# First half of the first weight unit as plain f32 products, and a new order of the first transfers

## The reference, cut to what matters

```python
def _rms_f32(xf, g):
    return xf * lax.rsqrt(jnp.mean(xf * xf, axis=-1, keepdims=True) + EPS) * g.astype(jnp.float32)

def hybrid_mixer(h, w_in, w_gate2, b_gate, g_gla, g_q, g_k, w_out):
    proj = h @ w_in
    cuts = np.cumsum([GLA_DK, GLA_DK, GLA_DV, GLA_DV, GLA_GATE_RANK, SB_D, SB_D])
    gq, gk, gv, gr, glr, sq, sk, sv = jnp.split(proj, cuts, axis=-1)
    ...
# in the first block, layer 0
hn = rms_norm(h, mix_norm[layer])
mix = hybrid_mixer(hn, hy_w_in[i], ...)
```

## Time and profile before

| | |
|---|---|
| median of 3 runs | 1041.45 us (1041.06 to 1042.47) |
| the profiled execution | 1040.92 us |
| its span, from first to last instruction | 1039.1 us |
| PE busy | 98% of the span |
| VectorE, ScalarE, GpSimd busy | 64%, 49%, 7% |
| mean granted clock of TensorE | 0.997 |
| first product of unit 0 | at 10.51 us |

### The profile page before, as it was taken

One profiled execution on the slowest core, in us unless ns is written; L12 is line 12 of the kernel. 1 busy time (PEld: TensorE's weight loads), 2 busy tenths in 40 slices (PEclk: granted clock), 3 DMA queues, 4 the chain that ended last, 5 costly groups with the idle time before them and its releaser, 6 DMA issues.

```text
span 1039.1 us, 15941 instructions
## 1 busy us (share of the span) xinstructions
PE 1013.4 (98%) x6789; PEld 869.5 (84%) x6796; DVE 668.1 (64%) x758; ACT 513.6 (49%) x598; POOL 72.1 (7%) x88
## 2 busy tenths in 40 slices
PE   9999999999999999999999999999999999999996
PEld 6996888888888986988989888899658888888885
DVE  6565578676768776768876666254589765455444
ACT  5567564344446325653544345454467464434434
POOL 0000100000000000001111000000148000000002
PEclk9999999999999999999999999999999999999998
DMA  7642457667664752458788775323000445545551
GB/s 266 214 163 81 153 194 276 230 227 246 211 242 164 230 171 83 163 186 304 284 299 277 269 270 208 122 81 122 1 1 2 151 155 202 191 174 201 176 189 41
DMA packets 33756, 187.60 MB, mean 181 GB/s; under 512 B 3744, under 2 KB 7584, under 8 KB 15136
## 3 DMA queue, kind: packets, MB, share of 16 engines
q1 hardware_dynamic: 25488, 155.08, 43.0%
q0 software_dynamic: 7344, 27.79, 7.5%
q10 hardware_dynamic: 864, 3.87, 1.0%
HBM read 181.61 MB, written 1.05 MB: 176 GB/s over the span
## 4 chain that ended last, share of the span: by engine, by line
PE 87%; DVE 7%; ACT 3%; DMA 2%; issue 1%; SPq 0%; DVEq 0%; ACTq 0%
PE PS L603 11%; PE PS L605 11%; PE PS L604 11%; PE PS L285 10%; PE PS L287 10%; PE PS L286 10%; PE PS L1175 2%; DMA raw<-wstream 2%; PE PS L670 2%; PE PS L668 2%; PE PS L669 2%; PE PS L636 1%; ACT w_hi L268 1%; DVE w_lo L272 1%; PE PS L1409 1%
## 5 line engine op out<-in xcount | busy, mean ns | idle before, releaser
L272 DVE TENSOR_TENSOR w_lo<-raw,w_hi 128x2048 fp32r<-128x2048 f32 x138 | 316.2, 2292 | 191.1 <-ACT w_hi L268 191.0
L268 ACT ACTIVATE w_hi<-raw 128x2048 fp32r<-128x2048 f32 x140 | 267.5, 1912 | 157.9 <-DMA raw<-wstream 68.1
L603 PE MATMUL PS<-w_hi,a_hi 128*128 128x512 f32 x512 | 203.1, 397 | 0.0
L605 PE MATMUL PS<-w_hi,a_lo 128*128 128x512 f32 x512 | 199.8, 390 | 0.0
L604 PE MATMUL PS<-w_lo,a_hi 128*128 128x512 f32 x512 | 199.7, 390 | 0.0
L285 PE MATMUL PS<-a_hi,w_hi 128*128 128x256 f32 (+1 forms) x512 | 154.8, 302 | 0.4 <-DVE a_lo L471 0.4
L286 PE MATMUL PS<-a_lo,w_hi 128*128 128x256 f32 (+1 forms) x512 | 151.6, 296 | 0.0
L287 PE MATMUL PS<-a_hi,w_lo 128*128 128x256 f32 (+1 forms) x512 | 151.6, 296 | 0.0
L605 PEld LDWEIGHTS PS<-w_hi,a_lo 128*128 128x128 f32 x512 | 96.1, 188 | 20.6
L603 PEld LDWEIGHTS PS<-w_hi,a_hi 128*128 128x128 f32 x512 | 96.3, 188 | 19.0 <-DVE w_lo L272 0.3
L604 PEld LDWEIGHTS PS<-w_lo,a_hi 128*128 128x128 f32 x512 | 96.4, 188 | 18.3
(11 more groups left out here) (375 smaller groups left out, 1401.8 us busy)
## 6 DMA issues: line engine op xcount, KB each, us to landing
raw<-wstream SPq DMA_DIRECT2D x141, 1024.0 KB, 4.8
modraw<-wmod POOLq DMA_DIRECT2D x48, 512.0 KB, 4.9
U<-CU SPq DMA_DIRECT2D x28, 142.0 KB, 2.8
cst<-cst ACTq DMA_DIRECT2D x1, 1632.0 KB, 9.3
mlw<-mlw ACTq DMA_DIRECT2D x1, 1280.0 KB, 5.4
X<-xT SPq DMA_DIRECT2D x2, 512.0 KB, 5.1
raw<-wstream SPq DMA_DIRECT2D x2, 512.0 KB, 7.8
CROW<-crow POOLq DMA_DIRECT2D x1, 1024.0 KB, 5.5
```

Source lines behind the costliest of these rows:

```text
L268: nc.scalar.activation(w_hi[:, slot, :], raw[:, rslot, :], ACT.Copy).then_inc(S("hi_done"), 1)
L272: dve.tensor_tensor(w_lo[:, slot, :], raw[:, rslot, :], w_hi[:, slot, :].bitcast(F32), ALU.subtract).then_inc(S("lo_done"), 1)
L603: nc.tensor.matmul(out, a_hi[:, k, src, ts], wh, start=k == 0, stop=False, skip_group_check=True)
L605: i = nc.tensor.matmul(out, a_lo[:, k, src, ts], wh, start=False, stop=k == KT - 1, skip_group_check=True)
```

## The change

- **Products.** PE makes 6 instead of 10 idle products. Then, for tiles 0 to 3 of unit 0, it makes plain f32 products: stationary is HN (X times the gain, made by VectorE in two instructions), moving is `raw` itself. Each pair of tiles waits for its part of HN and for its quarter of the unit. The ranks come behind them, and then unit 0 goes on from tile 4 in the split form. The two quarter conversions on ScalarE and the two quarter subtractions on VectorE for this half go away.
- **Transfers.** SP asks for X as tiles 0-1, 2-3 and 4-7, and for unit 1. ScalarE asks for the first parameters and for unit 0 in a quarter, a quarter and a half. The other parameters and `cst` are asked for after ScalarE's four pairs of `a_hi` tiles, `csb` after a wait for `cst`.
- **Waits.** SP waits for the ranks before it asks for unit 2, which overwrites the buffer that the plain products read. ScalarE waits for `cst` before `csb` and the squares. The semaphore `memset_done` is now called `dve_start`, `par_rest` is counted in `par_loaded`, and `csb_loaded` in `cst_loaded`.

```diff
@@ wait_x
-                eng.wait_ge(S(f"x_loaded{j // 2}"), 16)
+                eng.wait_ge(S(f"x_loaded{min(j, 2)}"), 16)
@@ sync
-            for j in range(2):
-                sp.dma_start(X[:, 4 * j:4 * j + 4, :].rearrange("p k t -> p (k t)"),
-                             A["xT"][:, 4 * j * T:(4 * j + 4) * T]).then_inc(S(f"x_loaded{j}"), 16)
-            for e, name in enumerate(("raw_first", "raw_loaded0")):
-                cols = slice(e * UNIT // 2, (e + 1) * UNIT // 2)
-                sp.dma_start(raw[:, 0, cols], raw_ap(0)[:, cols]).then_inc(S(name), 16)
+            for j, (a, b) in enumerate(((0, 2), (2, 4), (4, 8))):
+                sp.dma_start(X[:, a:b, :].rearrange("p k t -> p (k t)"), A["xT"][:, a * T:b * T])\
+                    .then_inc(S(f"x_loaded{j}"), 16)
             sp.dma_start(raw[:, 1, :], raw_ap(1)).then_inc(S("raw_loaded1"), 16)
...
+                if u == RAW_SLOTS:
+                    sp.wait_ge(S("gla_mm"), GLA_MM["ranks"])
                 sp.wait_ge(S("lo_done"), u - RAW_SLOTS + 1)
@@ tensor
-            pe.wait_ge(S("memset_done"), 1)
-            idle_products(2, 10)
-            pe.wait_ge(S("memset_done"), 5)
+            pe.wait_ge(S("dve_start"), 1)
+            idle_products(2, 6)
+            for k in range(KT // 2):
+                pe.wait_ge(S("dve_start"), 5 + k // 2)
+                pe.wait_ge(S(("raw_first", "raw_second")[k // 2]), 16)
+                for t in range(2):
+                    nc.tensor.matmul(PS[:, 4, t * T:(t + 1) * T], HN[:, k, t * P:(t + 1) * P],
+                                     raw[:, 0, k * 256:(k + 1) * 256], start=k == 0 and t == 0, stop=False,
+                                     skip_group_check=True)
+            pe.wait_ge(S("dve_start"), 7)
             for k in range(KT):
-                pe.wait_ge(S(f"x_loaded{k // 4}"), 16)
+                pe.wait_ge(S(f"x_loaded{min(k // 2, 2)}"), 16)
...
-                for k in range(KT):
+                for k in range(0 if u else KT // 2, KT):
                     if k == 0:
-                        pe.wait_ge(S("first_lo"), 3 if u else 1)
-                    if k == 2:
-                        pe.wait_ge(S("first_lo"), 3 if u else 2)
+                        pe.wait_ge(S("first_lo"), 1)
@@ scalar
-            act.dma_start(par[:, N_PAR0:], A["par"][:, N_PAR0:]).then_inc(S("par_rest"), 16)
+            for a, b, name in ((0, 4, "raw_first"), (4, 8, "raw_second"), (8, 16, "raw_loaded0")):
+                act.dma_start(raw[:, 0, a * P:b * P], raw_ap(0)[:, a * P:b * P]).then_inc(S(name), 16)
             table(LN_EXP)
...
-            for j in range(3):
+            for j in range(4):
                 first_tiles(j)
-            act.wait_ge(S("raw_first"), 16)
-            for e in range(2):
-                cols = slice(e * UNIT // 4, (e + 1) * UNIT // 4)
-                nc.scalar.activation(w_hi[:, 0, cols], raw[:, 0, cols], ACT.Copy).then_inc(S("first_hi"), 1)
-            first_tiles(3)
+            act.dma_start(par[:, N_PAR0:], A["par"][:, N_PAR0:]).then_inc(S("par_loaded"), 16)
+            act.dma_start(cst, A["cst"]).then_inc(S("cst_loaded"), 16)
             half_hi(0, 1)
-            act.dma_start(cst, A["cst"]).then_inc(S("cst_loaded"), 16)
             half_hi(1, 0)
             half_hi(1, 1)
-            act.dma_start(csb, A["csb"]).then_inc(S("csb_loaded"), 16)
+            act.wait_ge(S("cst_loaded"), 16)
+            act.dma_start(csb, A["csb"]).then_inc(S("cst_loaded"), 16)
@@ vector
             dve.wait_ge(S("par_loaded"), 16)
+            for j in range(2):
+                wait_x(dve, 0, j)
+                dve.tensor_tensor(HN[:, 2 * j:2 * j + 2, :], X[:, 2 * j:2 * j + 2, :],
+                                  prm("mixn0", 2 * j, 2).unsqueeze(2).to_broadcast([P, 2, T]), ALU.mult)\
+                    .then_inc(S("dve_start"), 1)
             dve.tensor_tensor(WGL.rearrange("p (k m) -> p k m", k=KT),
...
-            for j in range(3):
+            for j in range(4):
                 folded_lo(dve, 0, j)
-            for e in range(2):
-                cols = slice(e * UNIT // 4, (e + 1) * UNIT // 4)
-                dve.wait_ge(S("first_hi"), e + 1)
-                dve.tensor_tensor(w_lo[:, 0, cols], raw[:, 0, cols], w_hi[:, 0, cols].bitcast(F32), ALU.subtract)\
-                    .then_inc(S("first_lo"), 1)
-            folded_lo(dve, 0, 3)
             half_lo(0, 1)
```

More of the change, by code:

```diff
@@ L1528, in _ @@
             act.dma_start(par[:, 0:N_PAR0], A["par"][:, 0:N_PAR0]).then_inc(S("par_loaded"), 16)
-            act.dma_start(par[:, N_PAR0:], A["par"][:, N_PAR0:]).then_inc(S("par_rest"), 16)
+            for a, b, name in ((0, 4, "raw_first"), (4, 8, "raw_second"), (8, 16, "raw_loaded0")):
+                act.dma_start(raw[:, 0, a * P:b * P], raw_ap(0)[:, a * P:b * P]).then_inc(S(name), 16)
             table(LN_EXP)
-            act.wait_ge(S("memset_done"), 3)
+            act.wait_ge(S("dve_start"), 3)
             act.wait_ge(S("par_loaded"), 16)
@@ L1567, in _ @@
             act.wait_ge(S("gla_act"), 1)
-            act.wait_ge(S("par_rest"), 16)
+            act.wait_ge(S("par_loaded"), 32)
             def copy_proj(u):
@@ L1984, in _ @@
         def _(dve):
[L1985 to L1989, removed]
-            dve.wait_ge(S("par_loaded"), 16)
+            dve.memset(zero, 0.0).then_inc(S("dve_start"), 1)
+            dve.memset(epsc, EPS).then_inc(S("dve_start"), 1)
+            dve.memset(RESET, 1.0).then_inc(S("dve_start"), 1)
+            dve.wait_ge(S("dve_start"), 3)
+            dve.memset(RESET.rearrange("p (m c) -> p m c", c=CHUNK)[:, :, 0:1], 0.0).then_inc(S("dve_start"), 1)
+            dve.wait_ge(S("par_loaded"), 16)
+            for j in range(2):
[3 more added lines that the diff above has]
+                    .then_inc(S("dve_start"), 1)
             dve.tensor_tensor(WGL.rearrange("p (k m) -> p k m", k=KT),
@@ L1993, in _ @@
                               prm("mixn0", 0, KT).unsqueeze(2).to_broadcast([P, KT, 16]), ALU.mult)\
-                .then_inc(S("memset_done"), 1)
+                .then_inc(S("dve_start"), 1)
             def half_lo(u, e):
                 cols = slice(e * UNIT // 2, (e + 1) * UNIT // 2)
-                dve.wait_ge(*((S("hi_done"), u + 1) if e else (S("first_hi"), 3)))
+                dve.wait_ge(*((S("hi_done"), u + 1) if e else (S("first_hi"), 1)))
                 dve.tensor_tensor(w_lo[:, u, cols], raw[:, u, cols], w_hi[:, u, cols].bitcast(F32), ALU.subtract)\
                     .then_inc(S(("first_lo", "lo_done")[e]), 1)
-            for j in range(3):
+            for j in range(4):
                 folded_lo(dve, 0, j)
-            for e in range(2):
-                cols = slice(e * UNIT // 4, (e + 1) * UNIT // 4)
-                dve.wait_ge(S("first_hi"), e + 1)
-                dve.tensor_tensor(w_lo[:, 0, cols], raw[:, 0, cols], w_hi[:, 0, cols].bitcast(F32), ALU.subtract)\
-                    .then_inc(S("first_lo"), 1)
-            folded_lo(dve, 0, 3)
             half_lo(0, 1)
@@ L2013, in _ @@
             fold_squares(dve, 0)
-            dve.wait_ge(S("par_rest"), 16)
-            dve.tensor_scalar(epsc[:, 1:2], prm("sbq"), 0.125, None, ALU.mult).then_inc(S("memset_done"), 1)
+            dve.wait_ge(S("par_loaded"), 32)
+            dve.tensor_scalar(epsc[:, 1:2], prm("sbq"), 0.125, None, ALU.mult).then_inc(S("dve_start"), 1)
             lo(dve, 2)
@@ L2029, in qk_norm @@
                 if j == 2:
-                    dve.wait_ge(S("memset_done"), 6)
+                    dve.wait_ge(S("dve_start"), 8)
                 dve.scalar_tensor_tensor(QKN[:, j * 512:(j + 1) * 512], PROJ[:, 8 + j, :],
@@ L2048, in _ @@
             dve.wait_ge(S("gla_step"), 1)
-            dve.wait_ge(S("memset_done"), 4)
+            dve.wait_ge(S("dve_start"), 4)
             dve.tensor_tensor_scan(CUM, RESET, LA, 0.0, ALU.mult, ALU.add).then_inc(S("gla_step"), 1)
@@ L2092, in _ @@
             i.then_inc(S("gla_out"), 1)
-            dve.wait_ge(S("csb_loaded"), 16)
+            dve.wait_ge(S("cst_loaded"), 32)
             md = sbmask.rearrange("p (b n) -> p b n", b=3)[:, 0:3:2, :].unsqueeze(1).to_broadcast([P, 2, 2, P])
@@ L2157, in _ @@
             ffn_dve(dve, 0, folded=True, behind=2, mods=0)
-            dve.memset(CU[:, :, 0:TAPS - 1], 0.0).then_inc(S("memset_done"), 1)
-            dve.memset(CU[:, :, TAPS - 1 + T:PADT], 0.0).then_inc(S("memset_done"), 1)
-            dve.wait_ge(S("memset_done"), 8)
+            dve.memset(CU[:, :, 0:TAPS - 1], 0.0).then_inc(S("dve_start"), 1)
+            dve.memset(CU[:, :, TAPS - 1 + T:PADT], 0.0).then_inc(S("dve_start"), 1)
+            dve.wait_ge(S("dve_start"), 10)
             def taps_laid(k):
@@ L2315, in _ @@
             dve.wait_ge(S("norm_hn"), 8)
[L2316 to L2319, removed]
+            dve.memset(RST64, 1.0).then_inc(S("dve_start"), 1)
+            dve.wait_ge(S("dve_start"), 11)
```

(2 more changed lines are left out.)

## The result

The changed kernel is slower: 1044.72 us median (9 runs) against 1041.45 (9 runs); the ratio is 1.0032, with a 95% interval of 1.0021 to 1.0042. One of the nine, 1738.9 us at a mean clock of 0.637, counts in that median but not in the ratio. The forecast was 1042.65, with a range up to 1044.3: the direction was right, but the loss was 3.3 us instead of 1.2.

A forecast was written before the change was run, and what follows sets the result against it. PE, busy 98% of the span, was taken as the bound, so only tile 4's start counted: 13.48 to 14.8, rounded to +1.2 us. Profiled 1040.92 became 1042.1; with 0.53 for the median, 1042.65, range 1040.6 to 1044.3.

The forecast's parts named there:

- Queues take turns row by row: Start transfers: two queues alternate rows on the 16 DMA engines, so unit 0's second half lands at 11.6, not 9.4.
- PE's own new work and not the supply ends last before tile 4: Start of unit 0: PE's work ends at 14.8, the supply of tile 4 at 14.0.
- the plain form is no gain on PE: Tiles 0 to 3 of unit 0: eight plain products take 3.5 us, 24 split passes 2.9.
- the forecast case: Start of PE: clock rises among the plain products, tile 4 +0.6 to +1.9 us; chance 0.45.
- rival (3): Plain products: clock stays at 1.2 GHz through them, +3.3 us, 1044.7; chance 0.12.
- part 3: PE's new work before tile 4: 7.0 us from 6.3, plus half the low-clock time, ends at 14.8.
- the middle, 9.3: PE's start: clock rise taken between 8.0 (work adds up over the pause) and 10.6 (counts anew).
- the upper bound of 15.4: PE's start: tile 4's time if the clock's count begins anew after the pause, rising at 10.6.
- part 1: Start transfers: unit 0's quarters land at 6.3 and 8.4, its second half at 11.6 against 10.3 before.
- the engines would be full: Start transfers: row turns of two queues priced without idle engine time, such as 0.24 us for 2 KB rows on both.
- tile 4 tells the whole: From tile 4 of unit 0 on: same PE work in both kernels, so its +1.2 us moves all later work.
- Part 4: Added waits: SP's wait before unit 2 is covered with 0.2 us over; ScalarE's wait for cst costs nothing.

The follow-up runs named there:

- e9: e1_warm with unit 1 asked for by ScalarE behind unit 0 instead of by SP; ratio to the kernel before 1.0014.
- e2_six_idle: The kernel before with 6 instead of 10 idle products; ratio to the kernel before 1.0004.
- e1_warm: The changed kernel with 18 instead of 6 idle products, so no pause before the first plain product; ratio to the kernel before 1.0028.
- e8_long_rows: e1_warm with X and unit 0's first half in 4 KB rows (512 KB transfers), still on two queues; ratio to the kernel before 1.0032.
- e4_plain: The kernel before with the plain products for tiles 0 to 3 added behind the ranks, own transfers kept; ratio to the kernel before 0.9999.
- e5_both: The kernel before with the later parameters asked for later and the plain products behind the ranks; ratio to the kernel before 0.9997.
- e10_csb_late: e1_warm with csb asked for after unit 2's conversion instead of before the squares; ratio to the kernel before 1.0017.
- e7_transfers: The kernel before with the change's transfers and their waits, but its own ten idle products and split products; ratio to the kernel before 1.0032.
- e3_defer: The kernel before with the 337 KB of later parameters asked for after ScalarE's four pairs of input tiles; ratio to the kernel before 0.9995.
- e11: The kernel before with 22 more idle products between the ranks and unit 0, a delay only; ratio to the kernel before 1.0039.
- e6: The changed kernel with X and the weights on SP's queue in order of need, and ten idle products; ratio to the kernel before 0.9997.

## Why the prediction was wrong

**What held.** Queues take turns row by row; unit 1 pushes unit 0's second half back (e9: 2.4 us); PE's own new work and not the supply ends last before tile 4; the plain form is no gain on PE; the clock is low behind the pause; waits of ScalarE and the two HN instructions cost nothing. The path was that of the forecast case, PE's start, then its 7 us, part of them at the low clock; two terms of its sum were too small. That the time came out at rival (3)'s 1044.7 is chance: there 1.2 us of start are missing, and all eight plain products at half rate make up for them.

**The first term: the clock in part 3.** "I take the middle, 9.3." The rise came at 12.1. Work before the pause did not count: the clock rose 4.6 us after the restart in the changed kernel and about as much after it in e2_six_idle, against 4.3 after the very start before. Taken from its start at 7.49, the sum of part 3 is right: 7.49 + 7.0 + (12.1 - 7.49) / 2 = 16.8, measured 16.95. So 0.8 of the 2.15 us that tile 4 came too late (16.95 against 14.8) are the clock's. The 4.3 us of one trace was also taken as a fixed number: with 18 unbroken products it was 4.1 in e1_warm and 5.8 in e8_long_rows.

The Trainium skill, "TensorE: Matmul & The Clock Gate", part 1, cited in the prediction, says that sustained activity releases the throttle. Taken as activity without a break, which the 4.6 us after the restart agree with, it leads to the upper bound of 15.4 and not to the middle.

**The second, and the larger: the landings in part 1.** The first quarter was forecast for 6.3 and came at 7.4, the second half for 11.6 and came at 13.0. The turns were right, and so was the price of a 2 KB row of X (50.2% of 2 us x 16 engines for 189 rows is 0.085 us). Wrong was that the engines would be full: from 5 to 7 us they were at 83%, and the 100 rows of each queue, on 16 engines in 2 us, make 0.32 us for a turn of one row each, where the forecast had 0.24. The late first quarter is the other 1.2 us of tile 4 (7.49 against 6.3).

**The premise that tile 4 tells the whole** held for the change, but isn't true in general. In e1_warm, e4_plain and e5_both tile 4 moved and unit 2 did not follow, or only in part; e10_csb_late frees it. Reckoned from unit 2's shift, every ratio of the table comes out within its interval; reckoned from tile 4's, that of e7_transfers (1.0018) does not. e3_defer shows that even unit 2 doesn't tell the whole. Part 4 named this limit ("if the landing takes more than 5.2 us, the excess shows in full") and gave it 0.2 us of slack. In the changed kernel itself the landing took 4.8 and it cost nothing; once the clock is put right, it is what shows.

**The range** reached to 1044.3 and left out most of (3) on a chance of 0.12. The clock's rise was bounded at 8.0 to 10.6 after a start at 6.3. An uncertainty of one microsecond in that start was missing, which shifts the rise and the end alike, and one of more than a microsecond in the time until the rise.

**Left open.** The fall of the clock near 110 us was seen in the profiles of the changed kernel, e1, e7, e8, e9 and e10, and not in the others. A late start alone did not bring it in the one profile of e11, and I have no experiment that tells what does. In the changed kernel's runs, the three with a mean clock of 0.997 took 1044.12 to 1044.34 and the five with less 1044.59 to 1046.0. The kernel before spreads in the same way: of its 32 runs beside e1_warm, the six with a mean clock of 0.998 took 1040.4 to 1041.3 and the four with 0.995 1042.2 to 1043.8. So the spread doesn't belong to the change alone, and one profile of each kernel can't tell how often the clock falls there. The fastest runs of both kernels, 1044.12 and 1040.47, are 3.65 us apart, about the 3.6 of unit 2.

How much of the engines' unused share is the short rows' and how much the two queues' was not separated either. From 3 to 5 and from 5 to 7 us the engines were at 87% and 83% in the changed kernel, at 90% and 94% in e6 (short and long rows, nearly all on one queue) and at 92% and 101% in e8 (long rows and the parameters, two queues).

## What to carry to other kernels

Splitting the first transfers over two queues let what was behind on one queue, here a unit of long rows that nobody needed yet, take every other turn from what was needed first (2.4 us in e9). Of the orders tried here, the weights on one queue in the order of need did best (the kernel before, e3 to e6). TensorE's filler work that stopped 1.7 or 3.6 us before the first real product did nothing for the clock: size it to the measured landing. And a gain at the start is only one if the next unit's request and landing move with it, and if no engine further on eats it up (e3_defer).

## What the runs showed of the hardware

Row-by-row turns of two queues held from 3 to 7 us: 189 rows against 181, then 100 against 100. The Trainium skill, "DMA: Bandwidth & Descriptors", in its section on queues, rings and completion order, has an engine drain a packet of several descriptors from one queue before it turns; with eight rows per engine and transfer that would have let whole transfers alternate. The landings here don't agree with it: 12.9 for unit 1 and 13.0 for unit 0's second half, where a whole transfer of either, taken first by every engine, would have come at least 8 x 0.155 = 1.2 us before the other (an estimate from the earlier trace rows). Not expected was that two queues, one of them with 2 KB rows, left a sixth of the engines' time unused and moved 0.53 MB in 2 us, while 4 KB rows on both moved 0.80 MB in the same stretch. Nor was it expected that the clock would rise after 4.1 us of unbroken products in one profile and after 5.8 in another.
